# Expert slots numbered by token tile first: a sparse gather that writes each tile's columns once, and an operand assembled from two runs

## The reference, cut to what matters

```python
pg_top, g_sel = lax.top_k(pg, 1)
pe_top, e_sel = lax.top_k(jax.nn.softmax(el, axis=-1), TOP_K_IN_GROUP)
w = pg_top * pe_top / jnp.sum(pe_top, axis=-1, keepdims=True)
...
hid = jax.nn.silu(jnp.einsum('td,edf->tef', t, w1)) * jnp.einsum('td,edf->tef', t, w3)
hid = hid * combine[..., None].astype(hid.dtype)
out = jnp.einsum('tef,efd->td', hid, w2)
```

## Time and profile before

| | |
|---|---|
| median of 3 runs | 1219.73 us (1217.83 to 1222.15) |
| the profiled execution's own time | 1220.48 us |
| its span in the profile | 1218.8 us |
| busy: PE, PEld, DVE, ACT, POOL | 1181.1, 889.0, 699.4, 372.2, 44.5 us |
| read from HBM | 333.93 MB |

### The profile page before, as it was taken

How to read it: one execution, slowest core, us unless ns; L and a number is a source line. 1 busy time by engine, 2 the same in 40 slices (tenths; PEclk the granted TensorE clock), 3 DMA queues, 4 the chain that set the end, 5 groups by cost and what they waited for, 6 DMA issues and landing times.

```text
span 1218.8 us, 18891 instructions
## 1 busy us (share of the span) xinstructions
PE 1181.1 (97%) x7274; PEld 889.0 (73%) x7274; DVE 699.4 (57%) x1028; ACT 372.2 (31%) x392; POOL 44.5 (4%) x59
## 2 busy tenths in 40 slices
PE   8999999999999999999999999999999999999996
PEld 7888888888888888888898888555455454455552
DVE  5778555554666767676886556543344444343445
ACT  5444433334344353543434443110001110000012
POOL 1000000001002021000000000000000000000002
PEclk9999999999999999999999999999999999999998
DMA  8665655655655555455677594999999999999996
GB/s 298 191 197 184 193 185 181 198 174 175 202 160 160 165 172 155 155 171 177 207 239 191 167 408 177 347 430 431 417 429 432 432 430 432 431 432 431 426 417 250
DMA packets 156827, 336.64 MB, mean 276 GB/s; under 512 B 11232, under 2 KB 135280, under 8 KB 143088
## 3 DMA queue, kind: packets, MB, share of 16 engines
q1 hardware_dynamic: 152208, 335.69, 74.5%
q10 hardware_dynamic: 4576, 0.37, 0.3%
HBM read 333.93 MB, written 2.11 MB: 276 GB/s over the span
## 4 chain that ended last, share of the span: by engine, by line
PE 80%; DMA 14%; DVE 2%; SPq 2%; issue 1%; POOL 1%; ACT 0%; POOLq 0%; DVEq 0%; ACTq 0%
PE ps L955 20%; PE ps L1261 13%; DMA w_b<-in_w_dram 13%; PE ps L985 11%; PE ps L958 10%; PE ps L988 5%; PE ps L1129 4%; PE ps L1291 4%; PE ps L1131 2%; SPq L574 2%; PE ps L1300 1%; PE ps L1215 1%; PE ps L1301 1%; DMA fin_g<-in_final_g_dram 1%; PE ps L930 1%
## 5 line engine op out<-in xcount | busy, mean ns | idle before, releaser
L1381 DVE TENSOR_TENSOR wsplit<-wraw,wsplit 128x2048 fp32r<-128x2048 f32 x119 | 274.8, 2309 | 177.0 <-ACT wsplit L678 177.0
L678 ACT ACTIVATE wsplit<-wraw 128x2048 fp32r<-128x2048 f32 x119 | 228.1, 1916 | 377.2 <-PE ps L958 197.3
L955 PE MATMUL ps<-act_split,wsplit 128*128 128x512 f32 x1024 | 323.4, 397 | 0.0
L1261 PE MATMUL ps<-w_a,xe_a 128*64 128x256 f32 x960 | 221.5, 387 | 15.6 <-DMA w_b<-in_w_dram 15.5
L958 PEld LDWEIGHTS ps<-act_split,wsplit 128*128 128x128 f32 x1024 | 192.3, 188 | 45.4
L1261 PE MATMUL ps<-w_b,xe_b 128*64 128x256 f32 x960 | 221.5, 387 | 0.0
L1261 PEld LDWEIGHTS ps<-w_a,xe_a 128*64 128x64 f32 x960 | 130.6, 139 | 102.7 <-DMA w_b<-in_w_dram 22.4
L958 PE MATMUL ps<-act_split,wsplit 128*128 128x256 f32 x1024 | 201.3, 278 | 0.0
L985 PE MATMUL ps<-wsplit,act_split 128*128 128x512 f32 x608 | 192.2, 397 | 0.1
L955 PEld LDWEIGHTS ps<-act_split,wsplit 128*128 128x128 f32 x1024 | 156.3, 189 | 2.3 <-issue 1.8
L988 PEld LDWEIGHTS ps<-wsplit,act_split 128*128 128x128 f32 x608 | 114.2, 188 | 27.0
(11 more groups left out here) (315 smaller groups left out, 1114.9 us busy)
## 6 DMA issues: line engine op xcount, KB each, us to landing
wraw<-in_w_in_dram SPq DMA_DIRECT2D x88, 1024.0 KB, 5.0
w_a<-in_w_dram SPq DMA_DIRECT2D x37, 2048.0 KB, 15.5
w_b<-in_w_dram SPq DMA_DIRECT2D x37, 2048.0 KB, 19.8
wraw<-in_w_out_dram SPq DMA_DIRECT2D x16, 1024.0 KB, 5.2
w_a<-in_w_dram SPq DMA_DIRECT2D x14, 1024.0 KB, 12.4
w_b<-in_w_dram SPq DMA_DIRECT2D x14, 1024.0 KB, 15.2
wraw<-in_w_branch_m_dram SPq DMA_DIRECT2D x8, 1024.0 KB, 5.2
wraw<-in_w_branch_a_dram SPq DMA_DIRECT2D x8, 1024.0 KB, 5.1
```

The costliest lines, as they stand in the source:

```text
L678: act.activation(wsplit[:, q % 2, :, 0], wraw[:, q % RAW], ACT.Copy).then_inc(rounded, 1)
L955: pe.matmul(banks[b], w[:, k, 0, b * P:(b + 1) * P], act_of(q, k), start=first and k == 0, stop=False)
L1261: last = pe.matmul(ps[b * SLOTS:(b + 1) * SLOTS, 2 * w, 0:FF], operands[b][:, k], w13[b][:, w, k], start=k == 0, stop=k == DC - 1)
L1381: dve.tensor_tensor(wsplit[:, q % 2, :, 1], wraw[:, q % RAW], wsplit[:, q % 2, :, 0].bitcast(F32), ALU.subtract).then_inc(split, 1)
```

## The change: what it does

Slots are numbered by token tile and then by expert. Tile 0's 256 pairs get slots 0 to 255 and tile 1's get 256 to 511. So `sel[:, t]` has 256 columns instead of 512, and the gather's matmuls of a tile have 256 columns and write only that tile's half of the bank. An expert's tokens are then two runs of columns: those of tile 0 and those of tile 1. The number of its tokens in tile 0 (`totals[:, 0]`) says where the second run begins. `starts[1]` is set back by that number, so that a window of 64 columns from it has the second run at its right place, and the operand is the second window with the first window's columns written over it where `slot < totals[:, 0, e]` (`keep`, a predicated copy).

Around it: the rank and total matmuls are two instead of five, `WARM_SELECT` is 3 instead of 6, ACT takes over three small copies and 12 of the 16 evictions, the first four channel groups of tile 0 are gathered ahead of tile 1's, the pair weights are worked out after the first operand, and the first pair's mix is transposed after part 1 instead of part 0. The diff, cut to its core:

```diff
-WARM_ROUTE, WARM_SELECT = 18, 6
-EARLY = 12
+WARM_ROUTE, WARM_SELECT = 18, 3
...
-        sel = sb("sel", [P, TT, PAIRS], F32R)
+        sel = sb("sel", [P, TT, T], F32R)
...
+        DVE_GATHERED = (1, 4, 7, 10)
+        def all_evicted(eng, end):
+            on_dve = sum(d < end for d in DVE_GATHERED)
+            eng.wait_ge(xg_act, end - on_dve)
+            eng.wait_ge(xg_dve, on_dve)
...
+            act.wait_ge(rank_read, 1)
+            act.activation(totals[:], ps[:, 1, 2 * EXPERTS:4 * EXPERTS].rearrange("p (t e) -> p t e", t=TT),
+                           ACT.Copy).then_inc(rank_read, 1)
...
+            for c in range(DC):
+                if c in DVE_GATHERED:
+                    continue
                 act.wait_ge(xg_summed, c + 1)
...
-            pe.matmul(ps[:, 1, 0:EXPERTS], before_r[:], mk[:, 0], start=True, stop=True)
...
+            pe.matmul(ps[:, 1, TT * EXPERTS:2 * TT * EXPERTS], ones_r[:], chosen, start=True, stop=True)
+            pe.matmul(ps[:, 1, 0:TT * EXPERTS], before_r[:], chosen, start=True, stop=True).then_inc(rank_summed, 1)
...
-                    last = pe.matmul(ps[:, gather_bank(c)], part[:, t, c], sel[:, t], start=t == 0 and k == 0,
-                                     stop=t == TT - 1 and k == 1)
+                    last = pe.matmul(ps[:, gather_bank(c), t * T:(t + 1) * T], part[:, t, c], sel[:, t], start=k == 0,
+                                     stop=k == 1)
...
                     if first and part < 2:
-                        pe.wait_ge(xg_act, (EARLY, DC)[part] // 2)
-                        pe.wait_ge(xg_dve, (EARLY, DC)[part] // 2)
                         pe.wait_ge(xe_ready, part + 1)
...
-                    if part == 0:
+                    if part == (1 if first else 0):
                         turn_mix(s)
...
+            def weights():
+                dve.wait_ge(gexp_done, 2)
...
+            def starts_of(i, c, places=((0, 0), (1, 0), (0, 1), (1, 1))):
+                return [dve.value_load(starts_i[0:1, t:t + 1, ds(i * 2 + b, 1), ds(c, 1)], min_val=0, max_val=PAIRS)
+                        for t, b in places]
+            def keep_of(i, c):
+                for b in range(2):
+                    last = dve.tensor_scalar(keep[:, b], iota_c[:, ds(c, 1)].rearrange("p c s -> p (c s)"),
+                                             totals[:, 0, ds(i * 2 + b, 1)], None, ALU.is_lt)
+                return last
...
-            def copy_tokens(starts_at, s):
+            def copy_tokens(starts_at, i, c, s):
                 dve.wait_ge(h_parts, s * PARTS + 1)
-                for b, at in enumerate(starts_at):
-                    dve.tensor_copy(xe[b][:], xg[:, :, ds(at, SLOTS)]).then_inc(xe_ready, 1)
+                steps_x.done(keep_of(i, c))
+                spare_slots = xg[:, :, PAIRS:]
+                for b in range(2):
+                    steps_x.done(dve.tensor_copy(spare_slots, xg[:, :, ds(starts_at[2 * b], SLOTS)]))
+                    dve.tensor_copy(xe[b][:], xg[:, :, ds(starts_at[2 * b + 1], SLOTS)])
+                    dve.drain()
+                    steps_x.done(dve.copy_predicated(xe[b][:], kept(b, DC), spare_slots))
+                    dve.sem_inc(xe_ready, 1)
+
+            def first_tokens(starts_at, half):
+                first_second, second_first, second_second = starts_at
+                ks = slice(half * (DC // 2), (half + 1) * (DC // 2))
+                all_evicted(dve, (half + 1) * (DC // 2))
+                dve.tensor_copy(xg[:, ks, PAIRS:], xg[:, ks, ds(first_second, SLOTS)])
+                dve.tensor_copy(window[:], xg[:, ks, ds(second_first, SLOTS)])
+                dve.tensor_copy(xe_first[:, ks], xg[:, ks, ds(second_second, SLOTS)])
+                dve.drain()
+                dve.copy_predicated(xg[:, ks, PAIRS:], kept(0, DC // 2), xg[:, ks, 0:SLOTS])
+                steps_x.done(dve.copy_predicated(xe_first[:, ks], kept(1, DC // 2), window[:]))
+                dve.sem_inc(xe_ready, 1)
...
-                second, = starts_of(0, 0, (1,))
-                gathered(1, EARLY)
-                dve.tensor_copy(xe_first[:, 0:EARLY], xg[:, 0:EARLY, ds(second, SLOTS)]).then_inc(xe_ready, 1)
-                gathered(EARLY + 1, DC)
-                dve.tensor_copy(xe_first[:, EARLY:], xg[:, EARLY:, ds(second, SLOTS)]).then_inc(xe_ready, 1)
+                first_starts = starts_of(0, 0, ((1, 0), (0, 1), (1, 1)))
+                steps_x.done(keep_of(0, 0))
+                first_tokens(first_starts, 0)
+                gathered(DVE_GATHERED[3:])
+                first_tokens(first_starts, 1)
+                weights()
                 make_mix(0, 0, 0)
```

More of the change, by code:

```diff
@@ L192, in layer @@
         ones = sb("ones", [P, P])
+        AT_UPTO = place["at"]
         upto = sb("upto", [P, P])
@@ L262, in layer @@
         sc = sb("sc", [P, 12, TT])
-        table = sb("table", [P, 2, EXPERTS])
+        table = sb("table", [P, TT, EXPERTS])
         oh = sb("oh", [P, TT, 2, EXPERTS])
@@ L391, in gather_bank, with evicted @@
             return (c + 2) % 8 if c < 14 else c - 12
+        DVE_GATHERED = (1, 4, 7, 10)
+        def evicted(c):
+            on_dve = sum(d <= c for d in DVE_GATHERED)
+            return (xg_dve, on_dve) if c in DVE_GATHERED else (xg_act, c + 1 - on_dve)
+        def all_evicted(eng, end):
+            on_dve = sum(d < end for d in DVE_GATHERED)
+            eng.wait_ge(xg_act, end - on_dve)
+            eng.wait_ge(xg_dve, on_dve)
         def by_most(eng, experts):
@@ L1193, in _ @@
             pe.wait_ge(mk_ready, 1)
-            pe.matmul(ps[:, 1, 0:EXPERTS], before_r[:], mk[:, 0], start=True, stop=True)
[L1195 to L1199, removed]
+            chosen = mk[:].rearrange("p t e -> p (t e)")
+            pe.matmul(ps[:, 1, TT * EXPERTS:2 * TT * EXPERTS], ones_r[:], chosen, start=True, stop=True)
+            pe.matmul(ps[:, 1, 0:TT * EXPERTS], before_r[:], chosen, start=True, stop=True).then_inc(rank_summed, 1)
             pe.wait_ge(rms_diag_ready, 1)
@@ L1221, in _ @@
                 pe.wait_ge(sel_ready, t + 1)
-                for c in range(8):
-                    if t == 0 and c == 6:
-                        pe.wait_ge(rank_read, 1)
+                for c in range(4):
                     gather(c, t)
-            for c in range(8, DC):
-                pe.wait_ge((xg_act, xg_dve)[c % 2], (c - (8 if c < 14 else 6)) // 2 + 1)
+            for c in range(4, DC):
+                if c == 6:
+                    pe.wait_ge(rank_read, 4)
+                if c >= 8:
+                    pe.wait_ge(*evicted(c - (8 if c < 14 else 6)))
                 for t in range(TT):
@@ L1330, in experts @@
                     return
-                hidden(0, 0, (xg[:, :, 0:SLOTS], xe_first))
+                hidden(0, 0, (xg[:, :, PAIRS:], xe_first))
                 turn(0)
@@ L1829, in _ @@
             for t in range(TT):
[L1830 to L1835, removed]
+                slots_t = iota_s[:, t * T:(t + 1) * T]
@@ L1847, in _ @@
[L1847 to L1851, removed]
-            steps.done(last)
-            dve.tensor_copy(starts_i[:], starts[0:1])
-            dve.tensor_copy(most_i[:], stat[0:1, 35:36]).then_inc(tab_ready, 1)
-            dve.memset(xg[:, :, PAIRS:], 0.0)
@@ new lines, in _ @@
+            gathered(DVE_GATHERED[:1])
+            dve.wait_ge(rank_read, 3)
+            dve.wait_ge(iotas, 2)
+            by_chunk = iota_c[0:1, :, 0:1].rearrange("p c s -> p s c").to_broadcast([1, EXPERTS, CHUNKS])
+            dve.tensor_tensor(starts[:, 0], table[0:1, 0].unsqueeze(2).to_broadcast([1, EXPERTS, CHUNKS]), by_chunk, ALU.add)
+            dve.tensor_tensor(tile_sum[:], totals[:, 0], totals[:, 1], ALU.add)
+            steps.done(dve.tensor_tensor(table[0:1, 1], table[0:1, 1], totals[0:1, 0], ALU.subtract))
@@ new lines, in _ @@
+            dve.tensor_reduce(stat[:, 35:36], tile_sum[:], AX.X, ALU.max)
+            steps.done(dve.tensor_tensor(starts[:, 1], table[0:1, 1].unsqueeze(2).to_broadcast([1, EXPERTS, CHUNKS]), by_chunk,
+                                         ALU.add))
+            steps.done(dve.tensor_scalar(starts_i[:], starts[:], float(PAIRS), None, ALU.min))
+            dve.tensor_copy(most_i[:], stat[0:1, 35:36]).then_inc(tab_ready, 1)
+            gathered(DVE_GATHERED[1:3])
+            steps_x = Steps(dve, dve_x)
@@ L1987, in experts @@
                 up(0)
-                copy_tokens(starts_of(1, 0), 1)
+                copy_tokens(starts_of(1, 0), 1, 0, 1)
                 make_mix(1, 0, 1)
@@ L1998, in pair @@
                     add(i - 1, (4, 5, 6, 7))
-                with steps_x.loop(0, N_PAIRS // 2 - 1, 4) as j:
+                with steps_x.loop(0, N_PAIRS // 2 - 1, 14) as j:
                     for n in (1, 2):
```

65 lines of the change are left out of this document (37 added, 28 removed).

## The result

The changed kernel takes 1267.34 us (median of 4 runs, 1265.96 to 1267.59), the kernel before 1220.11 in the same job: 1.0383 times as long, 95% interval 1.0370 to 1.0396. The forecast had the sign, and 11 of the 47 us.

The account below looks back on a forecast made before the run. It took a chain of gather, pair 0, 14 periods and a fixed tail as the bound. Pair 1 came 1.1 us earlier, 14 periods were 28.85 instead of 27.96: +11.4 on 1219.73 gave 1231, range 1219 to 1246.

Parts of the forecast that it names:

- The direction, and the place: Slower, chance 0.73: in the pairs, DVE's operand copies set the period, 28.85 us instead of 27.96, +11.4 us in all.
- their cover: Time before PE wants pair 2's copies from DVE: 3.8 us in the kernel before, plus what the weights are late.
- The front and the gather: Ahead of the pairs: earlier start and gather matmuls 0.22 to 0.237 us apart, limited by weight loads; gain 1.5 us.
- The chain: DVE's loads, masks and copies for the next pair's operand: ready 28.8 us behind the pair's first matmul instead of 22.5.
- What PE's wait costs: In each pair PE finishes its work at 26.32 us and then waits 2.5 us for DVE's operand.
- the 22.4 us of the earlier trace: Wait for weights in the pairs of the kernel before, 15 pieces, matched to 14 x 1.64 = 23 us.
- The hidden copies: Rival in the pairs: predicated copy at 0.69 us, under 0.75, keeps copies almost hidden; period 27.8, time 1221; chance 0.20.
- The slow one at 2.29: Rival in the pairs: predicated copy takes 2.29 us, period 31.0, +41.5, time 1261; chance 0.08.
- The gather did not halve: Rival at the gather: 0.11 us a matmul; 1229 with the slow loop, 1216 or less with copies hidden too, chance 0.07.
- The clock rival: Rival in pair 0: the clock stays low for half of its 14 us, +7, time 1238; chance 0.03.

## Why the prediction was right and wrong

- **The direction, and the place: right.** The copies of `copy_tokens` no longer fit under their cover, the loop from one first matmul to the next closes over DVE, and the waits for weights vanish. Shown by the waits of the changed kernel, and by the run with the chain alone in the kernel before.
- **The front and the gather: right.** Gain 2.1 for 1.5. `sel` is 0.35 and 0.48 us (0.36 and 0.48 forecast), the pace 0.22; part 1 did not stall. L1955 of pair 1 is at 789.20, less the 1.67 us of the later start 787.53, for 787.55 forecast. The load as the limit is shown by the run with neighbouring columns. Of the two rules that I had weighed, that of "SBUF — State Buffer", section "Door 1: The DMA port swizzle" in the Trainium skill (each new 16-byte line is charged) points the right way (0.22 us apart for every 16th column, at most 0.12 for neighbouring ones). That of "TensorE: Matmul & The Clock Gate", section "LDWEIGHTS (loading the stationary operand)", in the Trainium skill fits neighbouring columns (0.10 to 0.11 apart in the earlier trace rows, 107 ns stated) and not every 16th.
- **The chain: its size was off.** Forecast 28.80 behind the pair's first matmul, measured 29.83 in pair 1 (814.85 - 785.02) and 29.62 on average. Term by term in pair 1: the loads 2.81 behind the `add`s instead of 2.43; masks 0.55 for 0.62; the two experts 3.12 and 2.88, waits and drains within, and 0.20 until PE starts, 6.20 together, instead of 5.56, since a predicated copy is 1.30 and not 1.22, and each dependent step has 0.07 to 0.23 us between instructions where I had 0.06. In the later pairs the loads leave 2.42 to 2.57, about what I had, so that there nearly all of the excess is in the copies and between them. At 29.62 instead of 28.85, that is 11 us over 14 periods.
- **What PE's wait costs: the step that failed.** I wrote "PE is done with `rows(1)` at 26.32 and then waits 2.5 us", and took the wait at its own length. It also costs the clock: 1.68 us a pair on average (31.30 - 29.62, the run with PE kept busy; 30.53 - 28.84 between the pairs of the run with one load ahead). With the forecast's own chain the kernel takes 1251, not 1231: had the chain been right, 1231 and my range up to 1246 would still have been missed.
- **The evidence stood in the rows.** At pair 13 L1900 has 6.14 us of idle time where 1.63 is usual, and I read the 4.5 us as late weights. PE waited 2.60 of them. Of the other 1.9 the clock is 1.7. The sum over the pairs has the same fault: the 22.4 us of the earlier trace rows are waits of the weight-load line, and PE itself stood for 15.5. Four views of the kernel before show it: PE's line on the page, a matmul half a microsecond behind the wait before 1121.57, and windows behind the waits before 1033.91 and 1121.57.

```profile
L1261 PE MATMUL ps<-w_a,xe_a 128*64 128x256 f32 x960 | 221.5, 387 | 15.6 <-DMA w_b<-in_w_dram 15.5
```

```profile
1122.07 0.63 PE L1261 MATMUL ps<-w_a,xe_a 128*64 128x256 f32 x1
```

```profile
1033.00:1039.00 6.00, 5.09 (x40) 3.24 (x42) 1.62 (x4) 0.00 (x0) 0.00 (x0) 1.00 0.99 423
1121.00:1127.00 6.00, 5.43 (x33) 3.79 (x34) 0.29 (x1) 0.00 (x0) 0.00 (x0) 0.72 1.01 434
```

  Behind 2.60 us the clock is 0.72 on the mean of the 6 us, and it is the same behind the waits of 2.54 before 868.64 and 1063.14; behind the 2.53 before 1033.91 it stays at 1.00. A look at such windows would have put one more term into the sum, at most 28.85 + 1.7 = 30.55, and 1255; with three waits of four, 1249. That it falls behind every wait of 3 us is shown by the changed kernel alone, not by the kernel before.
- **The rivals.** The hidden copies: no, the predicated copy is at 1.30, above its limit of 0.75. The slow one at 2.29: no; that its 1261 is the nearest to 1267 is luck, since it gets there through another mechanism. The gather did not halve. The clock rival was right about what the clock can do, and put it ahead of pair 0, once, instead of into every period.

The sum for the 46.8 us: 14 x (28.85 - 27.96) = 12.5 as forecast, 14 x (29.62 - 28.85) = 10.8 for the chain, 14 x 1.68 = 23.5 for the clock.

## What to carry to other kernels

If a change makes the matrix engine wait once in each period of a closed loop, price the wait together with what the clock does behind it, read from windows behind waits of that length that the kernel already has. The same loss is harmless where a transfer stream sets the pace and becomes full cost where the loop closes over compute. Before an assembly chain is judged by its length, look which of its parts need nothing that is late: here moving four register loads across one instruction was worth 48 us.

## What the runs showed of the hardware that I had not expected

- **The cost of a wait has a jump.** Waits of 1.4 to 1.6 us in every pair cost nothing beyond themselves; 2.1 to 2.5 us cost 1.68 more in most pairs. Behind the waits of 2.7 us and more, those of the changed kernel and of the chain in the kernel before, the clock fell every time. Below that the length alone does not decide: in the run with one load ahead it fell behind a wait of 2.11 us (1205.53) and held behind 2.29 (842.79) and 2.13 (1146.41); in the kernel before with neighbouring columns it held behind 2.54 (950.75) and fell behind 1.98, which the expectation of the run with one load ahead had not counted. What else decides stays open. The wait of 1.98 and the window behind it:

```profile
1176.35 0.40 PE L1261 MATMUL ps<-w_a,xe_a 128*64 128x256 f32 x1 [1.98 <-DMA w_b<-in_w_dram]
```

```profile
1176.35:1182.35 6.00, 6.00 (x36) 4.29 (x37) 0.58 (x2) 0.00 (x0) 0.00 (x0) 0.72 1.01 425
```

- **Register loads on DVE's sequencer** cost some 0.7 to 0.8 us for each one more where nothing covers them: gaps of 0.98, 1.70 to 1.86 and 2.42 to 2.57 us for two, three and four (in pair 1 0.98, 2.06 and 2.80). Ahead of an instruction that waits for PE they are free.
- **A predicated copy** of 128x1024 fp32 takes 1.30 us (plain 0.69), of 128x512 0.72 to 0.76 (plain 0.43).
- **Weight loads with a stride** of 64 bytes hold up the path for 0.22 us, neighbouring ones for at most 0.12.
